# TensorE takes the retrieved rows of an expert FFN slot by slot instead of in pairs, with finer preparation pieces

## What is computed

```python
x = x + mix @ w_out                                   # rows of 1024 tokens and 64 sample tokens
# PEER, chunks of 128 tokens, 8 heads
q = (xc @ w_query).reshape(PEER_CHUNK, PEER_HEADS, 2, PEER_HALF)
s = einsum('thcd,hckd->thck', q, keys)                # 2 x 128 scores a head
top_s, top_i = top_k(s, 16)                           # then the 16 best of the 16 x 16 sums
best_s, best_j = top_k(cand_s, 16)
gate = softmax(best_s)
act = gelu(einsum('thkd,td->thk', u_table[idx], xc))
y = einsum('thk,thkd->td', gate * act, v_table[idx])  # 128 rows of u and of v for each token
```

## Time and profile before

| | us |
|---|---|
| median of 3 runs (lowest to highest) | 3195.45 (3191.93 to 3195.72) |
| the profiled execution's own time | 3197.71 |
| its span | 3195.9 |
| PE busy | 2242.0 (70%) |
| DVE busy | 2074.9 (65%) |
| POOL busy | 1376.1 (43%) |
| ACT busy | 941.7 (29%) |

### The profile page before, as it was taken

How to read it: one execution, slowest core, us unless ns; L and a number is a source line. 1 busy time by engine, 2 the same in 40 slices (tenths; PEclk the granted TensorE clock), 3 DMA queues, 4 the chain that set the end, 5 groups by cost and what they waited for, 6 DMA issues and landing times.

```text
span 3195.9 us, 28190 instructions
## 1 busy us (share of the span) xinstructions
PE 2242.0 (70%) x7587; PEld 781.2 (24%) x7587; DVE 2074.9 (65%) x5165; ACT 941.7 (29%) x3203; POOL 1376.1 (43%) x1265
## 2 busy tenths in 40 slices
PE   8997878766855685567656765676567756675676
PEld 4556633211211221112111211221112211221121
DVE  4556388786577557755785578556865676567654
ACT  4223244332223222322233222322332223222222
POOL 1331144445444444444444444444454444444443
PEclk9998998988987888889888987788888978898799
DMA  4214799999999999999999999999999999999997
GB/s 151 67 52 92 280 406 408 420 408 420 420 420 417 416 418 416 414 414 420 412 416 405 420 418 414 412 416 417 414 414 416 416 415 415 414 407 417 410 421 317
DMA packets 188944, 1203.53 MB, mean 377 GB/s; under 512 B 27625, under 2 KB 35353, under 8 KB 48321
## 3 DMA queue, kind: packets, MB, share of 16 engines
q0 software_dynamic: 157264, 1142.72, 87.2%
q1 hardware_dynamic: 31520, 59.01, 5.4%
HBM read 1188.20 MB, written 13.06 MB: 376 GB/s over the span
## 4 chain that ended last, share of the span: by engine, by line
DMA 47%; PE 24%; DVE 7%; issue 7%; ACT 4%; POOL 1%; POOLq 0%; DVEq 0%; ACTq 0%
DMA uv_ring<-in_uv_table,idx 42%; PE ACC L2233 15%; PE ZS L2152 6%; DMA early<-in_uv_table,idx 5%; DVE uv_ring L1993 3%; ACT dg L1703 2%; PE ZS L2067 1%; ACT dot L1696 1%; ACT dot L1683 1%; POOL uv_ring L1558 1%; PE ZS L2183 0%; PE ZS L2210 0%; PE ACC L2067 0%; DVE early L1993 0%; DVE ACC L2001 0%
## 5 line engine op out<-in xcount | busy, mean ns | idle before, releaser
L2233 PE MATMUL ACC<-uv_ring,dg 128*64 128x512 f32 x3924 | 1393.9, 750 | 781.5 <-ACT dg L1703 781.5
L1558 POOL DMA_INDIRECT uv_ring<-in_uv_table,idx x981 | 1153.1, 1175 | 1345.7 <-PE ACC L2233 1144.7
L1993 DVE CUSTOM_DVE_ANT_0 uv_ring<-uv_ring,xn 128x1024 f32<-128x1024 f32 x981 | 1199.0, 1225 | 760.8 <-DMA uv_ring<-in_uv_table,idx 755.9
L2233 PEld LDWEIGHTS ACC<-uv_ring,dg 128*64 128x64 f32 x3924 | 328.8, 157 | 1663.7 <-ACT dg L1703 1200.5
L1683 ACT ACTIVATE dot<-dot 128x2 f32<-128x2 f32 x544 | 110.6, 203 | 1894.6 <-DVE dot L1993 1894.4
L2233 PE MATMUL ACC<-early,dg 128*64 128x512 f32 x428 | 269.5, 764 | 102.6 <-ACT dg L1703 102.6
L1703 ACT ACTIVATE dg<-stack,dot 128x64 f32<-128x64 f32 x1088 | 319.2, 340 | 17.7
L1696 ACT ACTIVATE dot<-gate,dot 128x1 f32<-128x1 f32 x1088 | 261.2, 287 | 18.9
L2152 PE MATMUL ZS<-score_w,xnT 128*128 128x512 f32 x512 | 246.2, 622 | 0.0
L1993 DVE CUSTOM_DVE_ANT_0 early<-early,xn 128x1024 f32<-128x1024 f32 x107 | 131.2, 1226 | 93.8 <-DMA early<-in_uv_table,idx 93.6
L1558 POOL DMA_INDIRECT early<-in_uv_table,idx x107 | 125.6, 1174 | 153.2 <-PE ACC L2233 132.8
(11 more groups left out here) (364 smaller groups left out, 1702.3 us busy)
## 6 DMA issues: line engine op xcount, KB each, us to landing
uv_ring<-in_uv_table,idx POOLq DMA_INDIRECT x981, 14.2
score_w<-in_w_query SPq DMA_DIRECT2D x8, 1024.0 KB, 19.3
w_in<-in_w_in SPq DMA_DIRECT2D x8, 640.0 KB, 9.0
xt<-in_x SPq DMA_DIRECT2D x9, 512.0 KB, 4.9
xr<-in_x SPq DMA_DIRECT2D x9, 512.0 KB, 8.4
xc<-in_x_columns SPq DMA_DIRECT2D x8, 512.0 KB, 4.0
out_y<-S SPq DMA_DIRECT2D x8, 512.0 KB, 7.9
scratch_u<-pj SPq DMA_DIRECT2D x9, 256.0 KB, 2.1
```

The costliest lines, as they stand in the source:

```text
L1558: pool.indirect_dma_start(out=slot(t, s_), out_offset=None, in_=a["uv_table"], in_offset=bass.IndirectOffsetOnAxis(ap=idx[:, s_:s_ + 1], a ...
L1993: V.tensor_tensor_reduce(row, row, xn[:, g, :], 1.0, 0.0, ALU.mult, ALU.add, dot[:, s_:s_ + 1]).then_inc(dots, 1)
L2233: ins = nc.tensor.matmul(ACCS[t % 2][GT * g:GT * (g + 1), b, :], dg[:, n % DG, :], slot(t, n)[:, D + 512 * b:D + 512 * b + 512], start=Fal ...
```

## The change

TensorE now waits for one diagonal, sums that slot, releases it, does that slot's pieces, and goes to the next slot. The pieces are cut finer and put elsewhere: z of tiles from 2 on in two halves (slots (0, 9) and (0, 11)), the output projection in pieces of two matmuls at odd slots, the scores one matmul a slot over (2, 15) to (3, 14) and (4, 0) to (4, 15), and the two halves of the spread at slots 119 and 121. The pieces of VectorE, ScalarE and GpSimd that take the results move with them, by at most four slots, and `FIRST_STEPS` is redrawn. Number and shape of matmuls stay. The core of the diff:

```diff
-        SPREAD = NSLOT - KS + 9
+        SPREADS = (NSLOT - KS + 7, NSLOT - KS + 9)
...
-        FIRST_STEPS = ((0, 0), (8, 0), (60, 50), (69, 59), (71, 64), (80, 72), (84, 80), (88, 83), (NSLOT - 10, NSLOT))
+        FIRST_STEPS = ((0, 0), (8, 0), (56, 43), (60, 47), (72, 63), (73, 64), (85, 80), (NSLOT - 10, NSLOT))
...
-                                if (h, j) == (2, 8):
+                                if (h, j) == (2, 6):
                                     root("x", t_, ms_x, rs_x)
...
-                    elif at == (3, 2):
+                    elif at == (2, 14):
                         k["xn_turned"].of(act, t)
...
-                    elif at in ((3, 12), (5, 0)):
-                        n = "ab"[at == (5, 0)]
+                    elif at in ((4, 0), (5, 2)):
+                        n = "ab"[at == (5, 2)]
                         k[f"s_{n}"].of(act, t)
...
-                    elif at == (2, 8):
+                    elif at == (2, 7):
                         k["bot_done"].of(dve, t)
...
-                    elif h in (4, 5) and at != (5, 0) or at == (6, 0):
-                        n, i = ("a", j) if h == 4 else ("b", j - 1 if h == 5 else KS - 1)
+                    elif (4, 2) <= at <= (5, 1) or (5, 4) <= at <= (6, 3):
+                        n, i = ("a", KS * (h - 4) + j - 2) if at <= (5, 1) else ("b", KS * (h - 5) + j - 4)
...
-                    elif at == (7, 13):
+                    elif at == (7, 15):
                         nearest(EH - 1)
...
-                    elif t > 1 and at in ((1, 1), (1, 5)):
-                        top_product(t, j // 4)
+                    elif t > 1 and at in ((1, 1), (1, 3), (1, 5), (1, 7)):
+                        half = j // 2 % 2 * (AW // P // 2)
+                        top_product(t, j // 4, half, half + AW // P // 2)
...
-                    elif at in ((2, 1), (2, 4)):
-                        b = int(at == (2, 4))
+                    elif at in ((1, 13), (1, 15), (2, 1), (2, 3)):
+                        b, half = h - 1, int(at in ((1, 15), (2, 3))) * (SW // P // 2)
...
-                    elif at == (2, 11) and t > 1:
+                    elif at == (2, 8) and t > 1:
                         begin(t)
-                    elif at == (2, 15):
+                    elif at == (2, 12):
                         k["xn_done"].of(pe, t)
...
-                    elif (h == 3 and 3 <= j < 11) or (h == 4 and j < 8):
-
-                        i = j - 3 if h == 3 else j
-                        n, bank, part = "ab"[h == 4], i // 4, i % 4
+                    elif t > 0 and (2, 15) <= at <= (3, 14) or h == 4:
+
+                        i = j if h == 4 else KS * (h - 3) + j + 1
+                        n, bank, m = "ab"[h == 4], i // KD, i % KD
...
-                        for m in range(2 * part, 2 * part + 2):
-                            ins = nc.tensor.matmul(ZS[:, bank, :], xnT[:, m, :], score_w[:, c_:c_ + 4, m, :],
-                                                   start=(m == 0), stop=(m == KD - 1))
-                        if i == 7:
+                        ins = nc.tensor.matmul(ZS[:, bank, :], xnT[:, m, :], score_w[:, c_:c_ + 4, m, :],
+                                               start=(m == 0), stop=(m == KD - 1))
+                        if i == 2 * KD - 1:
                             k[f"s_{n}"].mark(ins)
...
-                def add_v(t, s_, groups, last):
-
-                    pe.wait_ge(diags, t * NSLOT + s_ + BATCH)
-                    for n in range(s_, s_ + BATCH):
-                        g = n % groups
-                        for b in range(2):
-                            ins = nc.tensor.matmul(ACCS[t % 2][GT * g:GT * (g + 1), b, :], dg[:, n % DG, :],
-                                                   slot(t, n)[:, D + 512 * b:D + 512 * b + 512],
-                                                   start=False, stop=last and n >= s_ + BATCH - groups)
-                        ins.then_inc(pv, 1)
+                def add_v(t, n, groups, last):
+
+                    pe.wait_ge(diags, t * NSLOT + n + 1)
+                    g = n % groups
+                    for b in range(2):
+                        ins = nc.tensor.matmul(ACCS[t % 2][GT * g:GT * (g + 1), b, :], dg[:, n % DG, :],
+                                               slot(t, n)[:, D + 512 * b:D + 512 * b + 512], start=False, stop=last)
+                    ins.then_inc(pv, 1)

                 def retrieve(turn, t):
                     for b in range(0, slots_of(turn), BATCH):
-                        add_v(t, b, 1 if turn == "samples" else GROUPS, b + BATCH == slots_of(turn))
-                        if turn == "first":
-                            late_heads(b // BATCH)
+                        groups = 1 if turn == "samples" else GROUPS
                         for s_ in range(b, b + BATCH):
+                            add_v(t, s_, groups, s_ >= slots_of(turn) - groups)
+                            if turn == "first" and s_ > b:
+                                late_heads(b // BATCH)
```

More of the change, by code:

```diff
@@ L1739, in _ @@
                     for j in range(KS):
+                        if (h, j) == (2, 14):
+                            for n in range(QUARTERS, 2 * QUARTERS):
+                                take_weights(n)
                         prepare(0, h, j)
@@ L1878, in prepare @@
                         number_pairs(slice(0, EH))
[L1879 to L1882, removed]
+                    elif h == 6 and 5 <= j < 5 + EH:
+                        for stage in (0, 1) if j % 2 == 1 else (2, 3):
+                            best16(stage, head_candidates((j - 5) // 2 * 2))
+                    elif at == (6, 13):
                         chained()
@@ L1887, in prepare @@
                         k["best_shifted"].of(dve, t)
-                    elif at == (6, 12):
+                    elif at == (6, 14):
                         dch_(pairwise(top_f, cid, ALU.add))
-                    elif at >= (6, 14) and at <= (7, 12):
-                        e = 0 if h == 6 else 1 + j // 2
+                    elif h == 7 and j < KS - 1:
+                        e = j // 2
                         if j % 2 == 0:
@@ L2063, in _, with product @@
             def _(pe):
-                def product(bank, b, left, right):
-                    for n in range(SW // P):
+                def product(bank, b, left, right, n0=0, n1=SW // P):
+                    for n in range(n0, n1):
                         ins = nc.tensor.matmul(bank[:, b, :], left[:, n, :], right[:, n, 512 * b:512 * b + 512],
@@ L2069, in product, with top_product @@
                     return ins
-                def top_product(t, b):
-                    if b == 0:
+                def top_product(t, b, n0=0, n1=AW // P):
+                    if b == 0 and n0 == 0:
                         if t == 0:
@@ L2083, in top_product @@
                             k["zb_done"].of(pe, t)
-                    ins = product(top_bank(t), b, attention(t), w_top)
-                    if b:
+                    ins = product(top_bank(t), b, attention(t), w_top, n0, n1)
+                    if b and n1 == AW // P:
                         k["top_done"].mark(ins)
@@ L2125, in prepare @@
                             k["zb_done"].of(pe, 0)
-                        ins = product(product_bank(t), b, yT, w_bot)
-                        if b:
+                        ins = product(product_bank(t), b, yT, w_bot, half, half + SW // P // 2)
+                        if at == (2, 3):
                             k["bot_done"].mark(ins)
-                    elif at == (2, 11) and t > 1:
+                    elif at == (2, 8) and t > 1:
                         begin(t)
-                    elif at == (2, 15):
+                    elif at == (2, 12):
                         k["xn_done"].of(pe, t)
@@ L2247, in retrieve @@
                                 prepare(*prep)
-                            if s_ == SPREAD and turn != "samples":
+                            if s_ in SPREADS and turn != "samples":
                                 if turn != "eighth":
```

34 lines of the change are left out of this document (16 added, 18 removed).

## The result

The change takes 3202.9 us in the median of 8 runs (3200.22 to 3206.22), the kernel before 3195.24 in 8 runs on the same chip (3191.93 to 3196.67). The ratio is 1.0026 [1.0016, 1.0035]: slower by 7.7 us where 16 were forecast. The profiled execution of the change took 3200.22 us, its fastest; that of before, 3197.71, was above all of its timed runs.

The account below looks back on a forecast made before the run. DMA, moving gathers at about 420 GB/s, was taken as the bound. Steady tiles' 10 us plus the first tile's 6, all else 0, made 16 us on 3195.5, so 3212 us, with eight in ten between 3186 and 3237.

Parts of the forecast that it names:

- Price of a score slot: PE in the score stretch: one sum plus one score matmul takes 1.87 + 1.05 = 2.92 us, above the DMA's 2.491.
- The rival in which the sums overlap across a score matmul: PE score slots: sums still overlap, PE needs 2.0 us a slot, time 3195; chance 0.25 together with the slack rival.
- Does the slack cover it: Steady tiles, slot 72: PE's backlog outlasts the gathers' slack by 0.4 us, plus 1.0 for low clock, landing taken as 7.1.
- 1.4 us for each of seven tiles ... is 10 us: Steady tiles 2 to 8: each ends 1.4 us later, 10 us in all, bounds 0 and 41 us.
- small DMA stalls spread over the tile: Steady tiles before the change: 5.4 us a tile beyond gathers and other transfers, 1.7 us of it in 40 slots.
- engines ahead had paused and the one behind had not: Low-rate score window before the change: rows still came every 2.491 us, so only DMA engines that were ahead paused.
- First tile, 6 us: First tile's score slots, eight buffers: 12 slots take 38.5 us against 29.9 of DMA; loss 6 us, between 2 and 10.
- Pieces, roots, indices at nothing: Moved work on VectorE, ScalarE, GpSimd and split pairs: 0, or 1 us a tile if PE's backlog does not cover VectorE.
- The short windows are a real loss: Windows at 393 and 387 GB/s cost 20 us over seven tiles; finer pieces win it, 3175; faster outcomes 0.15.
- The PE lead is spent far earlier: Steady tiles: landings cannot fall below 11.6 us, each loses 5.9 us, 49 us in all, 3245; chance 0.13.
- The slack takes it all: Landings get under 6 us or low clock is free; first tile loses 2 us, 3195 to 3198; 0.25 with overlap.
- the pitch rises to 329.5: Sign of being right: score pieces of successive tiles come about 329.5 us apart instead of 328.1.

Follow-up runs that it names:

- e1: The change with its finer, moved pieces, but TensorE takes both sums of every pair first, then both slots' pieces: 3193.3 us, ratio 0.9995.
- e2: The change with the sums in pairs in the first tile alone, steady tiles still slot by slot: 3197.86 us, ratio 1.0011.
- e8: The change itself timed and traced once more, nothing altered: 3202.15 us, ratio 1.0026.
- e7: The change with the sums in pairs in all tiles but the first, which stays slot by slot: 3199.44 us, ratio 1.0015.
- e10: The all-pairs version of the change (e1) timed once more, nothing altered: 3192.33 us, ratio 0.9993.
- e13: The change with the sums in pairs in the whole first tile and in slots 32 to 71 of all tiles, slot by slot elsewhere: 3192.41 us, ratio 0.9994.
- e5: e1 plus 1024 no-operations on SyncE in each tile after the first: 3193.24 us, ratio 0.9997.
- e9: e1 plus twenty always-met waits with no-operations on PE behind each of slots 64 to 99 of tiles 1 to 6: 3193.14 us, ratio 0.9992.
- e12: e1 with gathers in tiles 1 to 7 held back by one, two, then three sums from slots 44, 52, 60: 3206.93 us, ratio 1.0042.
- e4: The kernel before with eight ring buffers in every tile instead of nine in the steady ones: 3197.61 us, ratio 1.0013.
- e3: The change with eight ring buffers in every tile instead of nine in the steady ones: 3225.25 us, ratio 1.0107.
- e6: The kernel before with the slot-by-slot order alone, pieces left coarse and where they were: 3206.69 us, ratio 1.0042.

## Why the prediction was wrong

*Price of a score slot: right.* 2.92 us by the rows above, busy throughout and at clock 1.00; eight-record pairs elsewhere. The rival in which the sums overlap across a score matmul fell.

*Does the slack cover it: the right sum from two wrong terms.* The lateness at slot 72 was put at 0.4 + 1.0 = 1.4 us, and is 1.5 us (in the mean over the steady tiles 3.53 in the change, 2.07 before, 1.93 in e1). The four stations of the sum in tile 3 of the change are slot 32's product (T), slot 63's sum, slot 72's gather and its product:

```profile
1470.68 1.23 DVE L1993 CUSTOM_DVE_ANT_0 early<-early,xn 128x1024 f32<-128x1024 f32 x1 [1.24 <-DMA early<-in_uv_table,idx]
...
1563.10 1.93 PE L2234 MATMUL ACC<-uv_ring,dg 128*64 128x512 f32 x4
...
1565.81 0.95 POOL L1558 DMA_INDIRECT uv_ring<-in_uv_table,idx  x1 [1.97 <-PE ACC L2234]
...
1573.97 1.23 DVE L1993 CUSTOM_DVE_ANT_0 uv_ring<-uv_ring,xn 128x1024 f32<-128x1024 f32 x1 [0.71 <-DMA uv_ring<-in_uv_table,idx]
```

Slot 63's sum starts at T + 92.4, for T + 92.5 predicted, and the gather at T + 95.1, for T + 95.2; in all seven tiles it is the same within 0.1 us. So the 1.0 us for the low clock was nothing: slot 32's sum starts at T + 4.9 in every tile, after PE has waited for its diagonal (1.74 us in tile 3, the first row of the score stretch above). It was also put too high to begin with: a mean clock of 0.85, made of 1.00 and 0.5, is the low level for 30% of the time, not for half. What took its place is the landing, 7.9 us in the mean instead of 7.1, and 0.2 us until VectorE has caught up. That 1.4 was met is luck in this part.

*"1.4 us for each of seven tiles ... is 10 us": this step failed.* It counted a row that is late at slot 72 as a tile that is late at its end, and took the 5.4 us a tile of "small DMA stalls spread over the tile" as a constant. They are not: in the change the rest of a tile loses 4.8 to 5.1 us instead of 6.2 in e1. Of the 10 us, 4.6 remained by the medians (e2 against e1), between 2.7 and 5.5 by the other pairings (3202.15 - 3199.44; 3197.86 - 3192.33); in the traces the seven steady tiles are 0.8 us longer than in e1 in the change, 2.8 in e2 and 3.3 in e8. The sentence that engines ahead had paused and the one behind had not was in the prediction, drawn from the earlier trace rows; it was used to dismiss the low windows and never carried into the loss of the change. Whether it is the cause of the give-back is not shown, as said above.

*First tile, 6 us: right.* 6.1 by e7 against e1; in the traces 336.7 and 336.1 us for the change, 331.0 for before, and 329.4 and 330.6 for e1 and e10. The mechanism is the predicted one. PE has no gap from 568 to 636 us, and the sums and pieces of slots 73 to 84 take 632.05 - 593.60 = 38.45 us, for 38.5 predicted:

```profile
593.60 1.95 PE L2234 MATMUL ACC<-uv_ring,dg 128*64 128x512 f32 x8
...
632.05 3.65 PE L2234 MATMUL ACC<-uv_ring,dg 128*64 128x512 f32 x12
```

*Pieces, roots, indices at nothing: right within the error.* e1 and e10 put all of them together at -1.1 and -2.6 us. In the steady tiles VectorE waits 4.8 us at the longest for `S` (about 5 was named), which makes slot 69's product 2.7 us later than its row, and has caught up at slot 72. In the first tile it waits 5.5 and 6.0 us, which nobody had named; PE stays busy meanwhile.

*The rivals.* "The short windows are a real loss" fell: e1 moves 419 instead of 414 GB/s in slots 48 to 72, and its seven tiles are as long as before. "The PE lead is spent far earlier" fell with landings of 5.5 us and, at slot 72, 7.9. "The slack takes it all" is half true, for a reason it did not name.

*The forecast's cues.* "The mean rate sinks under 400 late in b" came; "the pitch rises to 329.5" did not: 2292.7 / 7 = 327.5 us in the change and 327.9 in e8, so that the sign of the slack (at or under 328 with score slots at 2.92) came. Products closer than 2.49 us came too, at slots 70 to 72, but only because VectorE makes up there for its wait at 69.

No version beats the kernel before by more than its error. Pairs with the finer pieces, all or in the score slots (e1, e10, e13), stand at 3192.3 to 3193.3, 8.9 to 10.6 us under the change and 1.1 to 2.6 under before. With e5 and e9, built on e1, all five lie 1.1 to 2.6 us under their kernel before, so a gain of 1 to 2 us is likely but not shown.

## What to carry to other kernels

Before separating two instructions that run side by side on TensorE, price the overlap: here a full-array matmul between two half-array sums made two slots cost 5.84 us instead of 4.08, more than the 4.98 us of the DMA. When DMA is the bound, don't price a late row at its lateness: compare tile with tile, since part of it can come back; but that credit is small (1.8 us a tile at the most here), and e12 lost more than it got. When a sum comes out right, check its terms: here one of 1.0 us was nothing, and another was 0.8 too small. A low mean rate in a window, and a high one, say little until the pitch of complete rows is set beside them.

## What the runs showed of the hardware that was not expected

- With some five gathers of 1.05 MB under way (e1), packets worth 2.2 to 2.6 later rows had landed before a row was complete; behind a stretch with 2.5 under way (the change) it was 0.8, and the rate 420 instead of 414 GB/s. With eight buffers in pair order (e4) it was 1.8, at 412 to 414.
- The fastest landing of a 1.05 MB gather in the steady tiles was 5.5 to 5.6 us in the change, e3 and e6, with nine or eight buffers; the change's second trace (e8) has 6.0. Over slots 66 to 73 of the change, with two to four more under way, the mean of a slot was 7.3 to 8.0.
- In 41 steps of e1's steady tiles a row came 0.8 to 1.15 us late, and 28 of them began within 4 us behind an 8 KB transfer of instructions, where chance gives about 5.
- The first product starts at 395.0 to 399.6 us over the traces, a spread of 4.6 us and more than most effects here; a single pair of profiles could not have told 4 us.
